# Two blocks in one launch: later request of half the tokens in the prologue, and results of the unnormed slabs taken after all normed eighths

## The chip, the cores and the metric

One core of one Trainium2 chip runs the kernel as a single program. The metric is the device time of one execution in microseconds (us); the lower the better. The core has five engines with queues of their own: PE (TensorE, the matmuls), DVE (VectorE), ACT (ScalarE), POOL (GpSimd) and SP (SyncE, which here only asks for transfers). They meet on semaphores alone.

## What is computed

Two transformer blocks over 512 tokens of width 1024, all in float32. The first has a gated causal convolution, an attention with three dilated windows and a gated feed-forward part. The second has a sparse-attention layer and a stick-breaking layer. The change touches the first norm and the first projection only:

```
h = rms_norm(x, norm1_g)              # x: 512 tokens x 1024
z = h @ w_in                          # 1024 x 7168
a_val, a_gate = z[:, :1024], z[:, 1024:2048]
a = a_val * sigmoid(a_gate)           # the "glu" part: 16 slabs of w_in
a = causal_depthwise_conv(a, conv_w, conv_b)      # 31 taps
...
```

## The kernel before

**Weights as a stream of slabs.** All weights come in one stream (`wstream`) of slabs of 128 x 1024 floats (512 KB), in the order in which they are used. A ring of four slots holds them in SBUF. A float32 product is made of three passes: each slab is kept as a high part `W_HI` and a remainder `W_LO`, and the activations likewise as `X_HI` and `X_LO`; the helper `mm3` issues high x high, high x low and low x high. For most slabs `W_HI` is loaded (POOL, L508), ACT or POOL writes its negative to `W_LO` (L1338 on ACT, function `negate`), and an accumulating transfer adds the slab again (POOL, L494), so that the remainder is left. `W_HI` of slab n may be asked for when slab n - 4 is done (`slab_done`).

**The tokens.** `X_T`, which shares its memory with `GATE_A` (so the profile says GATE_A), holds the tokens transposed: 1024 features as eight "eighths" k = 0..7 of 128 x 512. SP asks for them in four quarters of two eighths each (L454, 512 KB each), each with a semaphore of its own, `xt_in[0..3]`. The identity matrix (part of `CONST`, L453) is asked for just before the last quarter.

**The prologue.** The inverse norm of a token is known only when all tokens have come and their squares are summed. So that PE has work before that, the first four slabs (RAW = 4) are multiplied with unnormed tokens: ACT writes `RAW_HI` (= `O_HI`, L1324), DVE writes `RAW_LO` (= `O_LO`, L1887), and PE (`raw_slabs`, L946, L949, L954) leaves the results of slab n in PSUM bank n. These four slabs get their low parts from a second copy of the slab (`FIRST`, in `QKV[:, 2]`, L461 on SP) that DVE subtracts (L1915). ACT then squares the tokens (L1326), DVE adds the squares in pairs (L1894, L1925), PE sums over features (L970), and ACT, DVE and PE turn the sum into `INVERSE_NORM` (a part of `CONV_ROOT`).

**After the inverse norm is known** DVE has two jobs. One is per eighth: `x_normed(k)` (L1904) scales the eighth in place, ACT copies it to `X_HI` (L1343, `x_high`), and DVE subtracts to get `X_LO` (L1909, `x_low`). The other is per raw slab: `raw_tile(n)` (L1901) multiplies PSUM bank n by the inverse norm, stores it into `CONV` or `CONV_IN` and raises `tile_free`. Before the change the raw tiles stand between the eighths: tile 0 after eighth 3, tile 1 after eighth 5, tile 2 after eighth 7's scaling, tile 3 at the end.

**Slab 4 and on.** From slab 4 PE works on normed tokens (`f_phase("glu", ...)`, function `turn`, L521 to L523): eight eighths of three products each, with slab n in PSUM bank n mod 4. Before the first product of slab 4 it waits for bank 0, and before each eighth of slab 4 for that eighth of `X_LO`:

```
            pe.wait_ge(tile_free, t0 - upper if first else t0 + 4 * i + j - 3)
        for k in range(KT):
            if i == (1 if begun else 0) and j == 0:
                ready(k)            # x_lo >= k + 1
```

For slab 4 (i = 1, j = 0) the first wait is for one `tile_free` beyond the start value, and `raw_tile(0)` is what raises it.

**ACT's order at this place** is written by hand: negate slab 4, `X_HI` of eighths 0 and 1, negate slab 5, `X_HI` 2 to 5, negate slab 6, `X_HI` 6 and 7, then the sigmoids of raw tiles 0 and 2 (`raw_gate`, L1348), then negate slab 7:

```
            negate(SLOTS + 1)
            x_high(range(2, 6))
            negate(SLOTS + 2)
            x_high(range(6, KT))
            raw_gate(0)
            raw_gate(1)
```

`negate` waits until its slab has landed. After this place DVE runs the 31-tap convolution (L1968, L1972) beside PE's projections.

Of the kernel before, what the change touches and what calls it, by code (L numbers as in the profile page):

```python
# [110 lines left out]
RAW = 4  # L111
# [84 lines left out]
def program(nc, x, xt, wstream, consts, small, lnv, out):  # L196
    with ExitStack() as ctx:
# [5 lines left out]
        def sem(name):  # L203
            if name not in sems:
                sems[name] = ctx.enter_context(nc.semaphore(name))
            return sems[name]
# [198 lines left out]
        def o_part(k):  # L405
            return slice(k * P, (k + 1) * P)


        gains_in, small_in, const_in, xt_in = sem("gains_in"), sem("small_in"), sem("const_in"), [sem(f"xt_in{k}") for k in range(KT // 2)]
# [5 lines left out]
        def sml(name):  # L415
            return SMALLS[:, S_AT[name]]
# [30 lines left out]
        @block.sync  # L447
        def _(sp):
            sp.dma_start(sml("g1"), small[:, S_AT["g1"]]).then_inc(gains_in, 16)
            for k in range(KT // 2):  # L450
                if k == KT // 2 - 1:

                    sp.dma_start(ident, consts[:, C_AT["ident"]]).then_inc(xt_in[k], 16)  # L453
                sp.dma_start(X_T[:, 2 * k:2 * k + 2, :], xt[:, 2 * k * SEQ:2 * (k + 1) * SEQ]).then_inc(xt_in[k], 16)  # L454


            sp.wait_ge(xt_in[KT // 2 - 2], 16)
            for n in range(RAW):
                if n == 2:
                    sp.wait_ge(sem("first_in0"), 16)  # L460
                sp.dma_start(FIRST[:, n, :], wstream[n]).then_inc(sem(f"first_in{n}"), 16)  # L461
            sp.wait_ge(slab_done, 3)
            sp.dma_start(SMALLS[:, KT:], small[:, KT:]).then_inc(small_in, 16)

            for n in range(4):
                sp.wait_ge(slab_done, 8 + 6 * n)
                part = slice(P + n * (C_W - P) // 4, P + (n + 1) * (C_W - P) // 4)
                sp.dma_start(CONST[:, part], consts[:, part]).then_inc(const_in, 16)

            for k in range(KT):  # L470
                sp.wait_ge(sem("a_v_lo"), k + 1)
                sp.dma_start(X_AGAIN[:, :, o_part(k)], x[:, o_part(k)].rearrange("(t p) d -> p t d", p=P))\
                    .then_inc(sem("res_in"), 16)
            for t in range(TT):
                parts = 2 if t == TT - 1 else 1
                for n in range(parts):
                    c = slice(n * D // parts, (n + 1) * D // parts)
                    sp.wait_ge(sem("normed"), TT + t + n + 1)
                    sp.dma_start(out[t * P:(t + 1) * P, c], RESIDUAL[:, t, c]).then_inc(sem("stored"), 16)
            sp.wait_ge(sem("stored"), 16 * (TT + 1))  # L480
# [34 lines left out]
        def _(pe):  # L515
# [262 lines left out]
            def attention_out(_, last_scores, last_values, fill):  # L778
                s0, t0 = SLAB0["attn_out"], TILE0["attn_out"]

                def part(n, ks):
                    s = (s0 + n) % SLOTS
                    for k in ks:
                        w = slice(k * P, (k + 1) * P)
                        pe.wait_ge(sem("a_ol"), k + 1)
                        mm = mm3(PSUM[:, n, :], W_HI[:, s, w], W_LO[:, s, w], O_HI[:, :, o_part(k)], O_LO[:, :, o_part(k)],
                                 k == 0, k == KT - 1)
                    return mm

                fill(PAIRS, 0)  # L790
                last_scores()
                fill(PAIRS, 1)
                last_values()

                pe.wait_ge(sem("a_biased"), 8 * PAIRS)
                for n in range(KT):
                    if n == 2:
                        pe.wait_ge(tile_free, t0)
                    slab_ready(s0 + n)
                    part(n, range(KT)).then_inc(slab_done, 1)  # L800
# [821 lines left out]
        def _(dve):  # L1622
# [274 lines left out]
            def raw_tile(n):  # L1897

                dve.wait_ge(slab_done, n + 1)
                dst = CONV_IN[:, n // 2, CW - 1:] if n % 2 else CONV[:, n // 2, :]  # L1900
                dve.tensor_tensor(dst, PSUM[:, n, :], INVERSE_NORM, ALU.mult).then_inc(tile_free, 1)  # L1901

            def x_normed(k):
                dve.scalar_tensor_tensor(X_T[:, k, :], X_T[:, k, :], sml("g1")[:, k:k + 1], INVERSE_NORM,  # L1904
                                         ALU.mult, ALU.mult).then_inc(sem("x_normed"), 1)

            def x_low(k):
                dve.wait_ge(sem("x_hi"), k + 1)
                dve.tensor_tensor(X_LO[:, k, :], X_T[:, k, :], X_HI[:, k, :].bitcast(F32), ALU.subtract).then_inc(sem("x_lo"), 1)  # L1909
# [21 lines left out]
            for k in range(KT):  # L1931
                x_normed(k)
                if k:
                    x_low(k - 1)
                if k in (3, 5, 7):
                    raw_tile(k // 2 - 1)
            x_low(KT - 1)
            raw_tile(3)
            dve.wait_ge(small_in, 16)
            dve.tensor_scalar(half_gate_b[:, :], sml("gate_b"), 0.5, None, ALU.mult).then_inc(sem("filled"), 1)  # L1940

# [112 lines left out]
            for i in range(0, FT // 2):  # L2054
                for m in range(2):
                    for v in range(2):
                        b, n = 2 * m + v, 4 * m + 2 * v
# [340 lines left out]
```

## Time and profile before

| | us |
|---|---|
| median of 3 runs | 1546.37 (1546.09 to 1546.46) |
| the profiled execution | 1547.69 |
| its span, first to last instruction | 1545.8 |
| PE busy | 1513.5 (98%) |
| DVE busy | 927.6 (60%) |
| ACT busy | 525.5 (34%) |
| POOL busy | 539.9 (35%) |

The span is what the trace shows; the profiled execution's own time has 1.9 us around it. Busy times are unions of an engine's instructions. Matmuls are pipelined: one of 128 x 512 is shown 0.39 us long, and the next starts 0.23 us after it, so start times are the ones to read.

### The profile page before, as it was taken

The numbers are of one execution on the slowest core, as the hardware profiler recorded it, in microseconds if no ns is written. First come the engines' busy times: TensorE is split into PE (matmuls) and PEld (weight loads), VectorE is DVE, ScalarE is ACT, GpSimd is POOL, SyncE is SP. The second block draws the span as 40 slices with busy tenths as digits, with TensorE's granted clock in tenths as the row PEclk, the third lists the DMA queues.
The fourth block names the chain that finished last, engine by engine and source line by source line (L and its number), as shares of the span: only waits on it lengthen the run. The fifth ranks groups of instructions, "written<-read, shape, count | busy, mean of one in ns | idle before, by whom it ended". The sixth has DMA issues, their size and how long they took to land.

```text
span 1545.8 us, 19010 instructions
## 1 busy us (share of the span) xinstructions
PE 1513.5 (98%) x7390; PEld 1226.5 (79%) x7390; DVE 927.6 (60%) x1584; ACT 525.5 (34%) x1021; POOL 539.9 (35%) x654
## 2 busy tenths in 40 slices
PE   9999999999999999999999999999999989999996
PEld 7888888877788788888888887788777768778775
DVE  7999969378864334443410025896787351777765
ACT  5323334177741222222200012212777032444530
POOL 1222234411134444444444443344111344333221
PEclk9999999999999999999999999999999999999998
DMA  8999998844459888988888887788333768665655
GB/s 255 200 199 197 197 194 188 187 101 96 93 131 195 174 183 192 193 193 194 195 193 193 179 187 169 157 191 181 79 83 73 173 156 193 136 138 125 126 128 131
DMA packets 73689, 252.96 MB, mean 164 GB/s; under 512 B 7936, under 2 KB 12800, under 8 KB 73600
## 3 DMA queue, kind: packets, MB, share of 16 engines
q0 software_dynamic: 65952, 240.15, 71.9%
q1 hardware_dynamic: 7104, 9.50, 1.8%
q10 hardware_dynamic: 544, 2.10, 0.5%
q8 instruction: 59, 0.97, 0.3%
q14 instruction: 30, 0.25, 0.1%
HBM read 249.62 MB, written 2.10 MB: 163 GB/s over the span
## 4 chain that ended last, share of the span: by engine, by line
PE 90%; DVE 5%; DMA 3%; issue 1%; ACT 1%; POOL 0%; SPq 0%; DVEq 0%; ACTq 0%
PE PSUM L521 26%; PE PSUM L523 25%; PE PSUM L522 25%; PE PSUM L729 3%; PE PSUM L687 2%; PE PSUM L705 2%; DMA W_LO<-wstream 1%; PE PSUM L864 1%; PE PSUM L876 1%; DMA W_HI<-wstream 1%; PE PSUM L889 1%; PE PSUM L675 1%; PE PSUM L1066 1%; DVE PROBS L1694 1%; DVE HEAD_BIAS L1667 1%
## 5 line engine op out<-in xcount | busy, mean ns | idle before, releaser
L508 POOL DMA_DIRECT2D W_HI<-wstream x231 | 130.0, 563 | 844.7 <-PE PSUM L523 822.5
L521 PE MATMUL PSUM<-X_HI,W_HI 128*128 128x512 f32 x840 | 334.9, 399 | 1.1 <-DVE X_LO L1909 0.7
L523 PE MATMUL PSUM<-X_HI,W_LO 128*128 128x512 f32 x840 | 327.6, 390 | 0.0
L522 PE MATMUL PSUM<-X_LO,W_HI 128*128 128x512 f32 x840 | 327.6, 390 | 0.0
L494 POOL DMA_DIRECT2D W_LO<-wstream x227 | 204.2, 900 | 109.3 <-POOL W_LO L491 82.6
L521 PE MATMUL PSUM<-W_HI,X_HI 128*128 128x512 f32 x544 | 213.2, 392 | 2.9 <-DMA W_LO<-wstream 2.9
L491 POOL TENSOR_SCALAR W_LO<-W_HI 128x1024 fp32r<-128x1024 f32 x191 | 207.4, 1086 | 24.6 <-DMA W_HI<-wstream 21.3
L522 PE MATMUL PSUM<-W_LO,X_HI 128*128 128x512 f32 x544 | 211.8, 389 | 0.0
L523 PE MATMUL PSUM<-W_HI,X_LO 128*128 128x512 f32 x544 | 211.8, 389 | 0.0
L521 PEld LDWEIGHTS PSUM<-X_HI,W_HI 128*128 128x128 f32 x840 | 157.3, 187 | 42.7 <-issue 10.1
L523 PEld LDWEIGHTS PSUM<-X_HI,W_LO 128*128 128x128 f32 x840 | 157.4, 187 | 34.0
L522 PEld LDWEIGHTS PSUM<-X_LO,W_HI 128*128 128x128 f32 x840 | 157.5, 188 | 30.9
L1972 DVE SCALAR_TENSOR_TENSOR CONV<-CONV_IN,SMALLS,CONV 128x512 f32<-128x512 f32 x240 | 159.4, 753 | 0.0
L2066 DVE SCALAR_TENSOR_TENSOR GATE_A<-PSUM,SMALLS,GATE_A 128x511 f32<-128x511 f32 x88 | 65.9, 749 | 143.2 <-ACT GATE_A L1441 141.6
L521 PEld LDWEIGHTS PSUM<-W_HI,X_HI 128*128 128x128 f32 x544 | 102.1, 188 | 28.6 <-DMA W_LO<-wstream 3.7
L523 PEld LDWEIGHTS PSUM<-W_HI,X_LO 128*128 128x128 f32 x544 | 102.1, 188 | 21.3
L522 PEld LDWEIGHTS PSUM<-W_LO,X_HI 128*128 128x128 f32 x544 | 102.1, 188 | 20.8
L1441 ACT ACTIVATE GATE_A<-PSUM,SMALLS 128x512 f32<-128x512 f32 x44 | 34.3, 780 | 166.1 <-PE PSUM L523 165.4
L1195 ACT ACTIVATE PROBS<-PROBS,soft_stats 128x128 f32<-128x128 f32 (+3 forms) x128 | 71.0, 558 | 35.4 <-DVE soft_stats L1694 35.3
L1338 ACT ACTIVATE W_LO<-W_HI 128x1024 fp32r<-128x1024 f32 x36 | 38.2, 1061 | 124.9 <-DMA W_HI<-wstream 124.9
L521 PE MATMUL PSUM<-W_HI,FFN_HI 128*128 128x512 f32 x176 | 68.7, 390 | 0.0
L523 PE MATMUL PSUM<-W_HI,FFN_LO 128*128 128x512 f32 x176 | 68.5, 389 | 0.0
(253 smaller groups left out, 2402.7 us busy)
## 6 DMA issues: line engine op xcount, KB each, us to landing
W_HI<-wstream POOLq DMA_DIRECT2D x231, 512.0 KB, 3.9
W_LO<-wstream POOLq DMA_DIRECT2D x227, 512.0 KB, 5.6
GATE_A<-xt SPq DMA_DIRECT2D x4, 512.0 KB, 6.2
QKV<-wstream SPq DMA_DIRECT2D x4, 512.0 KB, 5.0
QKV<-x SPq DMA_DIRECT2D x8, 256.0 KB, 2.7
NORM_GAINS<-lnv ACTq DMA_DIRECT2D x2, 1024.0 KB, 6.7
out<-GATE_B SPq DMA_DIRECT2D x3, 512.0 KB, 2.6
CONST<-consts SPq DMA_DIRECT2D x4, 194.0 KB, 5.2
```

Source lines behind the costliest of these rows:

```text
L491: pool.tensor_scalar(W_LO[:, r, :], W_HI[:, r, :].bitcast(F32), -1.0, 0.0, ALU.mult, ALU.add)\
L494: pool.dma_start(W_LO[:, r, :], wstream[n], accum_op=ALU.add).then_inc(w_lo_in[r], 16)
L508: pool.dma_start(W_HI[:, n % SLOTS, :], wstream[n]).then_inc(w_hi_in[n % SLOTS], 16)
L521: pe.matmul(o, lh, rh, start=start, stop=False)
L522: pe.matmul(o, lh, rl, start=False, stop=False)
L523: return pe.matmul(o, ll, rh, start=False, stop=stop)
L729: mm = pe.matmul(PSUM[:, out_bank(a, i)[h], kb * P:], ATT_V[:, kb, h, :], part[:, h, r, :].rearrange("p b q -> p (b q)"), start=kb == 0 an ...
L1195: act.activation(p, p, ACT.Exp, scale=-1.0, bias=soft_stats[:, 0, q, h:h + 1], accum_out=soft_stats[:, 1 + i % 2, q, h:h + 1]).then_inc(se ...
L1338: act.activation(W_LO[:, r, :], W_HI[:, r, :].bitcast(F32), ACT.Copy, scale=-1.0).then_inc(sem("w_neg_act"), 1)
L1441: act.activation(FFN_CONV[:, 2 * m + v, :], PSUM[:, 2 * m + v, :], ACT.Identity, scale=SMALLS[:, bass.ds(i * 12 + (S_AT["fw"].start + (2 * ...
L1972: dve.scalar_tensor_tensor(acc, src, w, acc, ALU.mult, ALU.add).then_inc(step, 1)
L2066: ins = dve.scalar_tensor_tensor(FFN_CONV[:, b, d:], PSUM[:, b, 0:SEQ - d], w, FFN_CONV[:, b, d:], ALU.mult, ALU.add)
```

## The change

SP now waits for the first quarter of the tokens before it asks for the third; the identity and the fourth quarter stand behind that wait. On DVE the four raw tiles come after the last `x_low`.

```diff
@@ block.sync
             for k in range(KT // 2):
+                if k == 2:
+
+                    sp.wait_ge(xt_in[0], 16)
                 if k == KT // 2 - 1:
 
                     sp.dma_start(ident, consts[:, C_AT["ident"]]).then_inc(xt_in[k], 16)
@@ block.vector
                 x_normed(k)
                 if k:
                     x_low(k - 1)
-                if k in (3, 5, 7):
-                    raw_tile(k // 2 - 1)
             x_low(KT - 1)
-            raw_tile(3)
+            for n in range(RAW):
+                raw_tile(n)
```

The order of SP's first transfers before the change (`GATE_A<-xt` are the quarters, `CONST` the identity, `QKV<-wstream` the second copies of raw slabs):

```order
L449 DMA SMALLS<-small 128x8
L454 DMA GATE_A<-xt 128x1024 x3
L453 DMA CONST<-consts 128x128
L454 DMA GATE_A<-xt 128x1024
L461 DMA QKV<-wstream 128x1024 [waits xt_in2]
```

and of the change:

```order
L449 DMA SMALLS<-small 128x8
L457 DMA GATE_A<-xt 128x1024 x2
L457 DMA GATE_A<-xt 128x1024 [waits xt_in0]
L456 DMA CONST<-consts 128x128
L457 DMA GATE_A<-xt 128x1024
L464 DMA QKV<-wstream 128x1024 [waits xt_in2]
```

The same transfers are issued in the same order; the third has a wait. No other queue's order changes.

DVE's order from eighth 5 on, before the change (L1904 is `x_normed`, L1909 `x_low`, L1901 `raw_tile`):

```order
L1904 SCALAR_TENSOR_TENSOR GATE_A<-GATE_A,SMALLS,CONV_ROOT 128x512
L1909 TENSOR_TENSOR X_LO<-GATE_A,X_HI 128x512 [waits x_hi]
L1901 TENSOR_TENSOR CONV_IN<-PSUM,CONV_ROOT 128x512 [waits slab_done]
L1904 SCALAR_TENSOR_TENSOR GATE_A<-GATE_A,SMALLS,CONV_ROOT 128x512
L1909 TENSOR_TENSOR X_LO<-GATE_A,X_HI 128x512 [waits x_hi]
L1904 SCALAR_TENSOR_TENSOR GATE_A<-GATE_A,SMALLS,CONV_ROOT 128x512
L1909 TENSOR_TENSOR X_LO<-GATE_A,X_HI 128x512 [waits x_hi]
L1901 TENSOR_TENSOR CONV<-PSUM,CONV_ROOT 128x512 [waits slab_done]
L1909 TENSOR_TENSOR X_LO<-GATE_A,X_HI 128x512 [waits x_hi]
L1901 TENSOR_TENSOR CONV_IN<-PSUM,CONV_ROOT 128x512 [waits slab_done]
```

and of the change, from eighth 6 on (L1907 is `x_normed`, L1912 `x_low`, L1904 now `raw_tile`):

```order
L1907 SCALAR_TENSOR_TENSOR GATE_A<-GATE_A,SMALLS,CONV_ROOT 128x512
L1912 TENSOR_TENSOR X_LO<-GATE_A,X_HI 128x512 [waits x_hi]
L1907 SCALAR_TENSOR_TENSOR GATE_A<-GATE_A,SMALLS,CONV_ROOT 128x512
L1912 TENSOR_TENSOR X_LO<-GATE_A,X_HI 128x512 [waits x_hi] x2
L1904 TENSOR_TENSOR CONV<-PSUM,CONV_ROOT 128x512 [waits slab_done]
L1904 TENSOR_TENSOR CONV_IN<-PSUM,CONV_ROOT 128x512 [waits slab_done]
L1904 TENSOR_TENSOR CONV<-PSUM,CONV_ROOT 128x512 [waits slab_done]
L1904 TENSOR_TENSOR CONV_IN<-PSUM,CONV_ROOT 128x512 [waits slab_done]
```

`raw_tile(0)`, which stood before `x_normed` of eighth 4, now stands behind `x_low` of eighth 7. PE's order is the same before and after; the place where slab 4 begins on PE reads, in both but for line numbers:

```order
L521 MATMUL PSUM<-X_HI,W_HI 128x512 [waits x_lo,tile_free,w_lo_in0]
L522 MATMUL PSUM<-X_LO,W_HI 128x512
L523 MATMUL PSUM<-X_HI,W_LO 128x512
L521 MATMUL PSUM<-X_HI,W_HI 128x512 [waits x_lo]
L522 MATMUL PSUM<-X_LO,W_HI 128x512
```

Its first product waits for `tile_free`; nothing moved on PE itself.

## Rows read from the trace of the kernel before

**Rows 1.** The page: shares of the chain that ended last, by engine.
```profile
PE 90%; DVE 5%; DMA 3%; issue 1%; ACT 1%; POOL 0%; SPq 0%; DVEq 0%; ACTq 0%
```
**Rows 2.** Timeline of PE, 30 to 40.5 us (start, length, instruction, [idle before, releaser]).
```profile
30.77 1.98 PE L954 MATMUL PSUM<-O_HI,W_LO 128*128 128x512 f32 x8
32.58 0.39 PE L521 MATMUL PSUM<-X_HI,W_HI 128*128 128x512 f32 x1
...
36.43 0.39 PE L523 MATMUL PSUM<-X_HI,W_LO 128*128 128x512 f32 x1
37.27 0.50 PE L521 MATMUL PSUM<-X_HI,W_HI 128*128 128x512 f32 x1 [0.45 <-DVE X_LO L1909]
...
38.47 0.50 PE L521 MATMUL PSUM<-X_HI,W_HI 128*128 128x512 f32 x1 [0.24 <-DVE X_LO L1909]
...
39.27 0.39 PE L521 MATMUL PSUM<-X_HI,W_HI 128*128 128x512 f32 x1
```
**Rows 3.** Timeline of DVE, 24 to 41 us.
```profile
28.89 0.68 DVE L1901 TENSOR_TENSOR CONV<-PSUM,CONV_ROOT 128x512 f32<-128x512 f32 x1
...
36.52 0.69 DVE L1909 TENSOR_TENSOR X_LO<-GATE_A,X_HI 128x512 fp32r<-128x512 f32 x1 [1.89 <-ACT X_HI L1343]
37.13 0.69 DVE L1901 TENSOR_TENSOR CONV<-PSUM,CONV_ROOT 128x512 f32<-128x512 f32 x1
37.73 0.68 DVE L1909 TENSOR_TENSOR X_LO<-GATE_A,X_HI 128x512 fp32r<-128x512 f32 x1
...
39.60 1.29 DVE L1959 TENSOR_TENSOR CONV_IN<-CONV_IN,CONV 128x512 f32<-128x512 f32 x2 [0.51 <-ACT CONV L1348]
```
**Rows 4.** Timeline of ACT: the raw high parts, the squares, and the normed high parts.
```profile
7.58 3.93 ACT L1324 ACTIVATE O_HI<-GATE_A,SMALLS 128x512 fp32r<-128x512 f32 x6 [1.34 <-DMA GATE_A<-xt]
11.42 4.26 ACT L1326 ACTIVATE GATE_B<-GATE_A 128x512 f32<-128x512 f32 x8
...
34.91 1.06 ACT L1338 ACTIVATE W_LO<-W_HI 128x1024 fp32r<-128x1024 f32 x1 [2.74 <-DMA W_HI<-wstream]
35.87 1.14 ACT L1343 ACTIVATE X_HI<-GATE_A 128x512 fp32r<-128x512 f32 x2
```
**Rows 5.** Issues of slab 6's high part alone: count, KB, us from issue to landing.
```profile
W_HI<-wstream POOLq DMA_DIRECT2D x1, 512.0 KB, 7.2
```
**Rows 6.** Waits of PE over the whole span: waited for, us in total, times, longest.
```profile
PE PSUM L521 <- DMA W_LO<-wstream: 3.6, 3, 1.8
PE PSUM L811 <- DVE GATE_B L1845: 3.3, 1, 3.3
```
**Rows 7.** Waits of DVE from 40 to 300 us.
```profile
DVE QK_LO L1672 <- ACT QK_HI L1177: 18.1, 1, 18.1
DVE CONV_ROOT L1994 <- PE PSUM L996: 7.4, 1, 7.4
```
**Rows 8.** The four quarters of the tokens: us from issue to landing, least, median, most.
```profile
DMA to landing us min/median/max: 3.6/6.2/7.1
```
**Rows 9.** Stretches: PE, PEld, DVE, ACT, POOL busy, granted clock, DMA share, GB/s.
```profile
4.00:5.00 1.00, 1.00 (x7) 1.00 (x7) 0.00 (x0) 0.09 (x1) 0.00 (x0) 1.00 0.90 332
5.00:6.00 1.00, 1.00 (x11) 1.00 (x10) 0.33 (x1) 1.00 (x2) 0.00 (x0) 1.00 1.08 401
5.00:10.00 5.00, 3.86 (x23) 2.77 (x22) 3.07 (x5) 3.66 (x6) 0.55 (x1) 1.00 1.06 390
1536.00:1537.00 1.00, 0.00 (x0) 0.00 (x0) 0.96 (x3) 0.20 (x1) 0.00 (x0) 1.00 0.73 299
1537.00:1538.00 1.00, 0.00 (x0) 0.00 (x0) 0.96 (x3) 0.00 (x0) 0.00 (x0) 0.64 0.00 0
```
**Rows 10.** Timeline of SP and DVE in the prologue: quarters asked for, and the first squares added.
```profile
1.18 1.37 SPq L454 DMA_DIRECT2D GATE_A<-xt  x3
...
13.63 1.23 DVE L1894 TENSOR_TENSOR GATE_B<-GATE_B 128x1024 f32<-128x1024 f32 x1 [1.23 <-ACT GATE_B L1326]
```
**Rows 11.** The last matmul of the program.
```profile
1532.19 0.39 PE L523 MATMUL PSUM<-W_HI,O_LO 128*128 128x512 f32 x1
```

## Prediction

> **What bounds the kernel now.** I read the chain of the page first: 90% of the chain that ended last is PE [rows 1]. So a microsecond counts only where PE stands still, and PE's time lost once near the start is paid at the end unless a later wait takes it up. Next I read PE's timeline at the place of the change. PE ends the unnormed slabs at 30.77 + 1.98 = 32.75, and slab 4 begins at once, at 32.58 by start times; it runs six eighths, 18 products, and then stands briefly before eighths 6 and 7, which start at 37.27 and 38.47 [rows 2]. Slab 5 starts at 39.27. The spacing of products is (36.43 - 32.58) / 17 = 0.227 us.
>
> What holds eighths 6 and 7 is in the timelines of ACT and DVE. ACT is idle 2.74 us until slab 6 has landed, negates it at 34.91, and only then copies `X_HI` of 6 and 7 at 35.87 [rows 4]; slab 6's transfer took 7.2 us [rows 5]. DVE is idle 1.89 us for that copy, does `x_low(6)` at 36.52, raw tile 2 at 37.13 and `x_low(7)` at 37.73 [rows 3].
>
> **The change, part one: DVE's order.** Slab 4 writes bank 0, and PE may not begin it before `raw_tile(0)` has raised `tile_free`. Before, that tile ran at 28.89, 3.9 us ahead of need [rows 3]. Now it stands behind `x_low(7)`, which stands behind `x_low(6)`, which needs the ACT copy behind slab 6's landing. None of these waits for PE's slab 4, so nothing locks; PE stands. DVE now does `x_low(6)` at 36.52, `x_low(7)` at 37.13 and `raw_tile(0)` at 37.73, one step of 0.6 us each, as the three instructions there now [rows 3]. The tile takes the place of the old `x_low(7)`, after which PE started at 38.47; so PE starts slab 4 at about 38.47 too. Then come all 24 products, where before only three were left. The other 21 were done under the wait: 21 x 0.227 = **4.8 us** later. DVE is quicker through eighths 4 to 7 since tiles 0 and 1 are gone from between them (2 x 0.6 us), but that only makes it wait longer for ACT: worth nothing, and its cover is the landing of slab 6. Tiles 1, 2 and 3 follow at 0.6 us each, far ahead of slabs 5 to 7, which start 5.4 us apart. ACT's sigmoid of raw tile 2 waits for `raw_tile(2)`, now done some 1.2 us after 38.4, so negate of slab 7 and the convolution begin 0.8 to 0.9 us later; PE needs slab 7 only three slabs, 16 us, after slab 4's start, so that is hidden too.
>
> **Does it come back later?** PE's waits after this place are short and hang on things that PE itself released: the longest are 3.3 us for DVE at L811, and three for slabs (3.6 us in all), whose transfers are asked for when PE ends an earlier slab [rows 6]. The one long job that does not follow PE is the convolution on DVE; but DVE waits 7.4 us for PE behind it, and 18.1 us for ACT's copy of PE's result before the attention [rows 7], so PE was never waiting for it. Nothing absorbs the 4.8.
>
> **Part two: the later request.** Before, SP asks for three quarters in a row from 1.18 [rows 10]; the landings take 3.6 us for the first and 7.1 for the slowest [rows 8], so the first lands at about 4.8 and the fourth at 10.2. Now the third is asked for at about 4.9, the identity and the fourth behind it, at some 0.5 us each. ACT starts on the second quarter at 7.58, runs six copies without a break to 11.51, then the squares [rows 4], and DVE starts adding these at 13.63 after an idle 1.23 us [rows 10]. So the end of the raw copies passes one to one to everything behind it, slab 6's request included. Bounds: the best is that the second quarter lands as ACT ends the first, at 6.25, worth 1.3 us. The worst is that the third quarter again takes its median 6.2 us from the later request: it lands at 11.1 where ACT wants it at 7.58 + 1.31 = 8.9, a loss of 2.2. From the least transfer, 3.6 us, it lands at 8.5 and the fourth, asked for at 5.9, at 9.5, and nothing is lost. The row nearest is the traffic itself: between 5 and 10 us the engines move 390 GB/s at a full share [rows 9], and the same quarters and slab 0 (2.7 MB with the identity) must all go through before the fourth has landed. Holding two back does not make fewer bytes; and the second stood ahead of them on SP's queue already. I take **0**, with +-0.8.
>
> The Trainium skill (DMA: Bandwidth & Descriptors, Queues, rings and completion order) says that an engine consumes a ring's descriptors in order and goes round between the rings that have work. By that rule the held-back quarters could not have delayed the second, which is on the same ring, but only slab 0 on POOL's: PE's first product would start earlier, and the end of the copies would not move. It speaks against the change's first half, and the rows do not contradict it.
>
> **The clock.** PE would stand from 32.75 to 38.48, 5.7 us. The trace has two rows to set beside it: an idle 3.3 us at L811 [rows 6], where the granted clock stayed at full speed, and the end of the program. There the last matmul ends at 1532.58 [rows 11], the clock is still full between 1536 and 1537, and the mean of 0.64 in the next us [rows 9] says that it fell to 1.2 GHz 0.28 us into it: 4.7 us after the last matmul. A stand of 5.7 us is beyond that one fall, so I think a fall likelier than none. Its price: after the start the warm-up matmuls go at 7 a us until 5 us and at 11 then [rows 9], so the slow stretch was some 4 us after the first at about 1.1. Four us at half speed cost 2.0 us; if up to 1.0 us of the low clock (5.7 - 4.7) lies in the stand, 3 us are left, 1.5. Bounds 0.5 and 3 (the stretch at 1 us, or at 6). I take **1.5**.
>
> The Trainium skill (TensorE: Matmul & The Clock Gate, HAM oscillation) describes just this: a PE that waits for data between bursts is throttled and begins each burst at half rate. By it the time is 1.5 us longer than by the 3.3 us row, where nothing fell; the end of this trace agrees.
>
> **Sum.** 4.8 + 0 + 1.5 = 6.3 us on the profiled execution's 1547.69, so 1554.0. That execution is 1.3 us above the median of the runs; the delay is the same in both, so the forecast is 1546.37 + 6.3 = **1552.7 us**.
>
> **Rivals.** (a) *The stand without the fall of the clock.* For it: only one fall is in the trace, and 5.7 is not far beyond 4.7. Then 1546.37 + 4.8 = 1551.2. Chance 0.3.
> (b) *The later request works or hurts by much.* If the second quarter came 1.3 us earlier and the rest in time, the prologue gives back 1.3: 1551.4 with the fall, 1549.9 without. If the third comes late by 2.2, 1554.9. Against: the full traffic of [rows 9]. Both lie in the range; chance 0.06 together beyond what I allow above.
> (c) *Slab 6 lands early, and the result is not slower.* The stand is set by slab 6's 7.2 us. If it took 3.6 us, the least that 512 KB took in the prologue, ACT would be free for 6 and 7 as soon as DVE has scaled them, and `raw_tile(0)` would follow DVE's own chain: the last scaling ended at 36.52 - 1.89 = 34.6 [rows 3], now 1.2 sooner, at 33.4; three steps of 0.6 end at 35.2, and slab 4 ends 24 products on, at 40.7 instead of 39.3. That is +1.4, less up to 1.3 from the request: 1546.5 to 1547.8, within 0.2%. It decides from a landing some 2 us sooner. It ends faster by over 0.2% (over 3.1 us, about what a measurement can tell from no change) only if something else in the prologue shortens as well. Against it: the same accumulating transfers of slabs 4 and 5 run beside slab 6 in both orders. Chance 0.04 within, 0.02 faster.
> (d) *The order does not do what it says*, another semaphore releasing bank 0. DVE's tiles are the only ones that raise `tile_free` before slab 4, and PE's first product names it. I give it nothing of its own; it is in the 0.02 to 0.04 of (c).
>
> **Chances.** Forecast 0.58, (a) 0.3, (b) 0.06, (c) 0.06. The range reaches from (a) with 0.8 us of gain, 1550.4, to the forecast with a slow stretch of 5 us and a late quarter, 1554.6; that leaves (c) and the worst end of (b) out. Slower by over 0.2% (above 1549.5): 0.94; within 0.2%: 0.04; faster: 0.02.
>
> **What would show it.** PE idle once for 5 to 6 us before its first L521, released by DVE's L1904 tile; 24 products in a row after it without the two short stands; slab 5 starting near 44 instead of 39.27; a granted clock below 1.00 in the stretch around 36 to 42, and product spacing of about 0.45 us there, if the fall comes. ACT's squares starting at 11.4, give or take 0.8, would show that the request is worth nothing. Everything behind should be the old timeline, shifted. I am wrong if PE starts slab 4 before 36, if the shift at slab 5 is gone by 300 us, or if the squares move by over 1.5 us.

## The result, and the profile after

| | us |
|---|---|
| before, median | 1546.41 (4 runs, 1546.09 to 1546.68) |
| changed, median | 1555.62 (4 runs, 1555.08 to 1559.44) |
| ratio, 95% interval | 1.0063 (1.0050 to 1.0076) |
| the profiled execution, its span | 1555.32, 1553.4 |

The change is slower by 9.2 us, 0.6%. The forecast was 6.3 us slower, with a range up to 1554.6: the direction and the place were right, the size was not, and the result lies 1.0 us outside. Between the two profiled executions the difference is 7.6 us (1547.69 and 1555.32): that of the kernel before lies 1.3 us above its median, that of the change 0.3 under its own.

The page of the changed kernel: busy times, and the chain by engine. Against before PE is busy 4 us longer in a span 7.6 us longer, so part of the loss is PE standing and part is PE running slower.

```profile
PE 1517.6 (98%) x7390; PEld 1229.9 (79%) x7390; DVE 927.3 (60%) x1584; ACT 525.6 (34%) x1021; POOL 540.1 (35%) x654
...
PE 90%; DVE 5%; DMA 2%; issue 1%; ACT 1%; POOL 0%; SPq 0%; DVEq 0%; ACTq 0%
```

PE's timeline of the changed kernel around the start of slab 4 (L524 to L526 are what L521 to L523 were), which answers to [rows 2]:

```profile
32.26 1.98 PE L957 MATMUL PSUM<-O_HI,W_LO 128*128 128x512 f32 x8
38.84 0.72 PE L524 MATMUL PSUM<-X_HI,W_HI 128*128 128x512 f32 x1 [4.61 <-issue]
39.36 0.63 PE L525 MATMUL PSUM<-X_LO,W_HI 128*128 128x512 f32 x1
...
41.92 0.58 PE L525 MATMUL PSUM<-X_LO,W_HI 128*128 128x512 f32 x1
42.34 0.39 PE L526 MATMUL PSUM<-X_HI,W_LO 128*128 128x512 f32 x1
...
45.97 0.39 PE L524 MATMUL PSUM<-X_HI,W_HI 128*128 128x512 f32 x1
```

One stand of 4.6 us, then 24 products in a row, the first eight 0.43 us apart and the others 0.23. Slab 5 starts at 45.97 where it started at 39.27: 6.7 us later. The profile puts the stand's end down to "issue"; what ended it is in DVE's timeline of the same kernel (L1912 `x_low`, L1904 `raw_tile`), to be read beside [rows 3]:

```profile
36.84 1.29 DVE L1912 TENSOR_TENSOR X_LO<-GATE_A,X_HI 128x512 fp32r<-128x512 f32 x2 [1.88 <-ACT X_HI L1346]
38.06 0.68 DVE L1904 TENSOR_TENSOR CONV<-PSUM,CONV_ROOT 128x512 f32<-128x512 f32 x1
38.66 0.68 DVE L1904 TENSOR_TENSOR CONV_IN<-PSUM,CONV_ROOT 128x512 f32<-128x512 f32 x1
```

Raw tile 0 runs from 38.06 to 38.74, and PE starts at 38.84. DVE itself had waited 1.88 us for ACT, and ACT for slab 6. ACT's timeline of the changed kernel, beside [rows 4]:

```profile
8.30 2.72 ACT L1327 ACTIVATE O_HI<-GATE_A,SMALLS 128x512 fp32r<-128x512 f32 x4 [1.89 <-DMA GATE_A<-xt]
11.18 1.34 ACT L1327 ACTIVATE O_HI<-GATE_A,SMALLS 128x512 fp32r<-128x512 f32 x2 [0.16 <-DMA GATE_A<-xt]
12.43 4.26 ACT L1329 ACTIVATE GATE_B<-GATE_A 128x512 f32<-128x512 f32 x8
...
35.24 1.06 ACT L1341 ACTIVATE W_LO<-W_HI 128x1024 fp32r<-128x1024 f32 x1 [2.13 <-DMA W_HI<-wstream]
```

The squares start 1.0 us later than before (12.43 against 11.42): the second quarter came 0.7 us later (8.30 against 7.58) and the fourth once more let ACT wait. The 0.7 us need not come from the change: in e13 below, where the tokens are asked for as before, ACT starts on the second quarter at 8.48. Slab 6's negation starts 0.3 us later (35.24 against 34.91).

Stretches of the changed kernel (PE, PEld, DVE, ACT, POOL busy, granted clock, DMA share, GB/s):

```profile
38.00:39.00 1.00, 0.16 (x1) 0.19 (x2) 1.00 (x3) 0.86 (x2) 0.00 (x0) 0.95 1.11 242
39.00:42.00 3.00, 3.00 (x8) 2.32 (x9) 2.88 (x7) 1.98 (x3) 0.00 (x0) 0.50 0.76 141
42.00:43.00 1.00, 1.00 (x5) 0.82 (x4) 1.00 (x4) 0.00 (x0) 0.00 (x0) 0.85 0.09 20
...
1247.00:1254.00 7.00, 5.79 (x18) 4.91 (x19) 4.35 (x8) 2.27 (x5) 2.93 (x3) 0.52 0.94 202
```

The clock fell to half, 1.2 GHz, at 38.9, after PE had stood since 34.24, and was back 3.4 us later; slab 4 took 7.1 us where 24 products at 0.227 take 5.4. There is a second stretch at half clock that was not in the profile of before: around 1247 to 1254, around the end of the stand of 3.3 us in a late norm, which is as long as it was [rows 6].

The 6.7 us at slab 5 are thus made of 0.4 for the start (38.84, foreseen at 38.47), 4.6 for the products (24 x 0.227, less the 0.8 us that the last three took before) and 1.7 for the clock. From there to a stand of PE near 1183 us (1190 in the change) both kernels take 1143.7 us, and behind it the change loses another 0.9.

### The profile page after: what moved, and what is told of

Its sections match the earlier page's. It is cut to its first block, busy times and chain, and to the rows that moved or that the text cites. A ratio compares the mean times of both kernels' runs of the same rounds, so it can differ in the third digit from the quotient of the medians.

```text
span 1553.4 us, 19010 instructions
## 1 busy us (share of the span) xinstructions
PE 1517.6 (98%) x7390; PEld 1229.9 (79%) x7390; DVE 927.3 (60%) x1584; ACT 525.6 (34%) x1021; POOL 540.1 (35%) x654
## 4 chain that ended last, share of the span: by engine, by line
PE 90%; DVE 5%; DMA 2%; issue 1%; ACT 1%; POOL 0%; SPq 0%; DVEq 0%; ACTq 0%
PE PSUM L524 26%; PE PSUM L525 25%; PE PSUM L526 25%; PE PSUM L732 3%; PE PSUM L690 2%; PE PSUM L708 2%; PE PSUM L867 1%; PE PSUM L879 1%; PE PSUM L892 1%; PE PSUM L678 1%; DMA W_LO<-wstream 1%; DMA W_HI<-wstream 1%; PE PSUM L1069 1%; DVE PROBS L1697 1%; DVE HEAD_BIAS L1670 1%
## 5 line engine op out<-in xcount | busy, mean ns | idle before, releaser
L524 PE MATMUL PSUM<-X_HI,W_HI 128*128 128x512 f32 x840 | 335.5, 399 | 5.0 <-issue 4.6
L526 PE MATMUL PSUM<-X_HI,W_LO 128*128 128x512 f32 x840 | 328.1, 391 | 0.0
L524 PE MATMUL PSUM<-W_HI,X_HI 128*128 128x512 f32 x544 | 214.3, 394 | 1.4 <-DMA W_LO<-wstream 1.1
L526 PE MATMUL PSUM<-W_HI,X_LO 128*128 128x512 f32 x544 | 212.5, 391 | 0.0
L524 PEld LDWEIGHTS PSUM<-X_HI,W_HI 128*128 128x128 f32 x840 | 157.7, 188 | 46.6 <-issue 15.1
L526 PEld LDWEIGHTS PSUM<-X_HI,W_LO 128*128 128x128 f32 x840 | 157.8, 188 | 34.0
L524 PEld LDWEIGHTS PSUM<-W_HI,X_HI 128*128 128x128 f32 x544 | 102.7, 189 | 27.5 <-issue 3.3
L526 PEld LDWEIGHTS PSUM<-W_HI,X_LO 128*128 128x128 f32 x544 | 102.5, 188 | 21.6
L524 PE MATMUL PSUM<-W_HI,FFN_HI 128*128 128x512 f32 x176 | 68.7, 390 | 0.0
L525 PE MATMUL PSUM<-W_LO,FFN_HI 128*128 128x512 f32 x176 | 68.5, 389 | 0.0
```

The costliest lines, as they stand in the source:

```text
L524: pe.matmul(o, lh, rh, start=start, stop=False)
L525: pe.matmul(o, lh, rl, start=False, stop=False)
L526: return pe.matmul(o, ll, rh, start=False, stop=stop)
```

## The experiments

The experiments ran in four groups (e1 to e4, e5 to e8, e9 to e12, e13 to e16), each on one chip. The kernel before ran again in each group, and its medians were 1549.95, 1548.98, 1548.51 and 1548.05 us, with runs from 1545.6 to 1552.9; its first four runs, within 0.6 us, were at the low end of that. Each difference below is against the kernel before of the same group. With such a spread a median of 11 or 12 runs is good to 1 to 2 us, one of 5 or 6 runs to about 2, and a single profile shows one execution, not the typical one.

### e1: the later request alone

```diff
             for k in range(KT // 2):
+                if k == 2:
+
+                    sp.wait_ge(xt_in[0], 16)
```

> The kernel before with the later request of the third and fourth quarter alone. In the profile of the change the third unnormed slab was done 1.5 us later than before (slab 6 asked for at 29.18 against 27.69), but slab 6 landed only 0.33 us later. Theory A (the late prologue is hidden by slab 6's landing): +0.2 to +0.5 us, 1546.6 to 1546.9. Rival B (what the prologue loses is paid in full): +1.5 us, 1547.9. The forecast had it at nothing: 1546.4.

Measured: 1550.85 (12 runs) against 1549.95, +0.9, ratio 1.0009 (0.9998 to 1.0020). The median lies between A and B, and the interval holds zero. The profiled execution shows more: slab 5 starts at 42.37, 3.1 us later than in [rows 2]. PE's timeline and a stretch of e1:

```profile
12.96 0.50 PE L952 MATMUL PSUM<-O_LO,W_HI 128*128 128x512 f32 x1
15.28 0.50 PE L949 MATMUL PSUM<-O_HI,W_HI 128*128 128x512 f32 x1 [1.82 <-DMA W_HI<-wstream]
```
```profile
16.00:19.00 3.00, 3.00 (x10) 2.28 (x9) 3.00 (x4) 0.07 (x1) 0.77 (x2) 0.54 0.88 274
```

PE waits 1.8 us for slab 1, which landed at 15.2 (asked for at 8.36, 6.9 us), and the clock falls behind that stand. So slab 5 can be several microseconds late in one execution, while the median hardly moves.

### e2: DVE's order alone

```diff
-                if k in (3, 5, 7):
-                    raw_tile(k // 2 - 1)
             x_low(KT - 1)
-            raw_tile(3)
+            for n in range(RAW):
+                raw_tile(n)
```

> The kernel before with all four raw tiles behind the last x_low, tokens asked for as before. Theory A (the stand of PE is the whole thing): 4.8 us for 21 products no longer done under the wait, and 1.5 to 2 us if the clock falls in the stand of 5.7 us; slab 5 starts 6.3 to 6.7 us later; with a second fall at the layer norm near 1248 us, one more: 1552.7 to 1554.1. Rival B (half of the 9.2 us come from the late request): under 1551.5.

Measured: 1557.83 (5 runs) against 1549.95, +7.9, ratio 1.0052 (1.0040 to 1.0065). PE in e2's profile:

```profile
38.53 0.47 PE L521 MATMUL PSUM<-X_HI,W_HI 128*128 128x512 f32 x1 [4.58 <-issue]
```

The same stand, and a fall of the clock 0.7 us behind its end: slab 5 starts at 45.70, 6.4 us late. The order carries most of the loss. The 7.9 us are above both theories' numbers; e15 repeats it.

### e3: raw tile 0 left in its place, the others behind

```diff
-                if k in (3, 5, 7):
-                    raw_tile(k // 2 - 1)
+                if k == 3:
+                    raw_tile(0)
             x_low(KT - 1)
-            raw_tile(3)
+            for n in range(1, RAW):
+                raw_tile(n)
```

> The kernel before with raw tile 0 where it was, after the eighth 3, and only tiles 1 to 3 behind the last x_low. Theory A (only tile 0's place costs, since bank 0 is what slab 4 waits for): no stand of PE before slab 4, and x_low of eighth 7 one step of 0.6 us earlier since tile 2 no longer stands before it: -0.5 us, 1545.9. Rival B (the move of the tiles costs by itself, through slabs 5 to 7 or the later convolution): +0.5 us or more.

Measured: 1549.53 (12 runs) against 1549.95, -0.4, ratio 1.0003 (0.9993 to 1.0013), no difference. In its profile PE has no stand before slab 4, and slab 5 starts here:

```profile
38.93 0.39 PE L521 MATMUL PSUM<-X_HI,W_HI 128*128 128x512 f32 x1
```

That is 0.3 us before [rows 2]. It is one tile, the one that frees bank 0, that costs the time; the move of the other three costs nothing that these runs can tell.

### e4: the change, with PE kept busy in its stand

```diff
                 high(3, range(KT))
                 low(3)
+                for n in range(26):
+                    pe.matmul(PSUM[:, 7, 0:P], ONES, ONES, start=True, stop=True)
```

> The change with 26 matmuls of 128 x 128 on the matrix of ones into the unused bank 7 behind the last unnormed slab, some 4.7 us of work in a stand of 4.6 to 5.7 us, so that PE is busy there. Theory A (1.6 to 2 us of the change is the clock falling in the stand): no fall near 39 us, product spacing 0.227 from the start of slab 4, 1.4 to 2.0 us under the change, 1553.6 to 1554.2; the later fall near 1247 may come or go with the shift. Rival B (the slow first products of slab 4 are something else): 1555.6 as the change.

Measured: 1556.13 (5 runs) against 1549.95, +6.2. By its median this is theory B's number, but the kernel before, too, is 3.5 us higher in this group than in its first runs; the profile decides. PE and DVE in its profile:

```profile
33.48 5.96 PE L987 MATMUL PSUM<-QK_SQ 128*128 128x128 f32 x52
39.20 0.48 PE L524 MATMUL PSUM<-X_HI,W_HI 128*128 128x512 f32 x1
39.52 0.40 PE L525 MATMUL PSUM<-X_LO,W_HI 128*128 128x512 f32 x1
```
```profile
37.27 0.69 DVE L1906 TENSOR_TENSOR CONV<-PSUM,CONV_ROOT 128x512 f32<-128x512 f32 x1
```

The products run at full speed at once, so the slow first products of the change are the clock. But I had made the filling too long: raw tile 0 ended at 37.96 and PE came back only at 39.20, so this kernel pays 1.2 us for its own filling. Without that I estimate +5.0 (6.2 - 1.2).

### e5: the kernel before, once more

> The kernel before, once more, for a profile on the chip of this call. In the last call its runs went from 1546.0 to 1552.9 where the first four were within 0.6 us. Theory A (the spread is slab 1's landing in the prologue, 12.0 us in the first profile and 13.8 to 15.2 in three of the last four, and the clock falling in short stands that it survives in other runs): a span over 1546 comes with slab 1 after 13.5 us or with a granted clock of 0.50 somewhere between 10 and 1530 us. Rival B (this chip is slower throughout): the stretches between are longer, with neither.

Measured: 1549.62 (8 runs), the profiled one 1548.80 with a span of 1546.9. Two stretches of it:

```profile
536.00:539.40 3.40, 3.40 (x18) 3.30 (x17) 2.89 (x5) 3.00 (x6) 1.01 (x2) 0.50 0.97 261
1242.00:1246.20 4.20, 3.08 (x12) 2.85 (x13) 3.79 (x8) 2.18 (x5) 2.70 (x3) 0.59 0.88 182
```

The unchanged kernel has the clock falling too: behind two stands of 0.8 and 1.0 us in the norm near 535, and behind the 3.3 us one. In the first profile neither fell. Slab 1 landed at 14.0 instead of 12.0, and slab 5 started at 39.29 all the same. Theory A holds for this execution: 1.7 us are gone by 545 us, at the first of the falls.

### e6: the change again

The kernel is the change, as it was.

> The change on the chip of this call, for a comparison without a change of chip. Theory A (the stand with its clock is 6.5 to 7 us, the rest of the first 9.2 us was chance of the runs): 6.5 to 7.5 us over the kernel before. Rival B (9 us belong to the change on any chip): 8.5 us or more over it.

Measured: 1556.89 (6 runs) against 1548.98, +7.9, ratio 1.0056 (1.0041 to 1.0071). Between the theories. It is the +7.9 of e2 again, so this pair, from two groups, gives nothing to the request; e13 to e16 put both in one group. The stand ends at 38.17, slab 5 starts at 45.34, 6.05 us after e5's.

### e7: the kernel before with ACT's last two high parts ahead of slab 6's negation

```diff
-            x_high(range(2, 6))
-            negate(SLOTS + 2)
-            x_high(range(6, KT))
+            x_high(range(2, KT))
+            negate(SLOTS + 2)
```

> The kernel before with ACT's high parts of eighths 6 and 7 ahead of the negation of slab 6, so that they do not wait for its landing. Theory A (what holds eighths 6 and 7 is ACT's place behind slab 6): no stand of PE at 37 to 38 us, slab 5 starts 1.2 us earlier, 1.2 us under the kernel before. Rival B (DVE's own chain holds them): no gain over 0.3 us.

Measured: 1549.19 (12 runs) against 1548.98, nothing (0.9991 to 1.0008). PE in its profile at the start of slab 5, and 17 us later:

```profile
38.45 0.39 PE L521 MATMUL PSUM<-X_HI,W_HI 128*128 128x512 f32 x1
...
55.77 0.50 PE L521 MATMUL PSUM<-X_HI,W_HI 128*128 128x512 f32 x1 [0.84 <-DMA W_LO<-wstream]
```

Slab 5 is 0.84 us earlier than in e5, so A was right about what holds the eighths, and then PE waits 0.84 us for a slab's remainder at slab 8. In this execution the gain was given back to the stream of weights. The interval reaches from 1.4 us faster to 1.2 slower, so a part of the gain in other runs is not ruled out.

### e8: the change with the same move on ACT

> The change with the same move on ACT. Theory A (the stand's length is set by slab 6's landing by way of ACT): raw tile 0 ends some 1.9 us earlier, PE's stand is 2.7 us instead of 4.6 and the clock does not fall in it: 1.9 us, with the clock 3.5 us, under the change of this call. Rival B (the stand is set by DVE's chain of the eighths alone): the stand stays at 4.6 us and the time at the change's.

Measured: 1554.62 (6 runs) against 1548.98, +5.6, and 2.3 us under e6. PE in its profile:

```profile
36.74 0.47 PE L524 MATMUL PSUM<-X_HI,W_HI 128*128 128x512 f32 x1 [2.78 <-issue]
```

The stand is 2.8 us, as expected, and the clock does not fall in it (slab 4 takes 5.53 us). The length of the stand is set by slab 6's landing by way of ACT. The profiled execution, 1551.68, is the fastest of the six, 2.9 us under their median; what the clock did in the stands of the others is not known.

### e9 and e12: no falls in the later norms

e9 is the kernel before and e12 the kernel of e3, both with

```diff
                         if c == 0:
+                            for n in range((0, 0, 3, 4)[t]):
+                                pe.matmul(PSUM[:, 0, t * P:(t + 1) * P], ident, ident, start=True, stop=True)
                             pe.wait_ge(sem("x_scaled"), scaled + t + 1)
...
                 if t == 2:
+                    pe.wait_ge(tile_free, TILE0["out_a"] + 5)
+                    for n in range(12):
+                        pe.matmul(PSUM[:, 4, 0:P], ident, ident, start=True, stop=True)
                     pe.wait_ge(tile_free, TILE0["out_a"] + 8)
```

> The kernel before with extra matmuls of 128 x 128 on the identity, into parts of banks that are overwritten next, where PE stands in the later norms: 3 and 4 of them before the last two tokens' turns of the norm near 534 us (stands of 0.77 and 0.98 us), 12 in the stand of 3.3 us near 1240 us. Theory A (the runs of the kernel before that lie above 1546.5 lie there because the clock falls after these stands): no fall at 536 or 1243, the median 1.5 to 3 us under the kernel before of this call, and a narrower spread, near 1546. Rival B (the spread comes from transfers): the median and the spread as before.

> The kernel of e3 (raw tile 0 in its place, tiles 1 to 3 behind the last x_low) with the extra matmuls of e9. Theory A (x_low of eighth 7 one step of 0.6 us earlier): 0.3 to 0.5 us under e9, and so the fastest of all. Rival B (PE reaches eighth 7 no sooner than before because the unnormed slabs end later in most runs): the same as e9 within 0.3.

Measured: e9 1548.61 (11 runs) and e12 1547.89 (11 runs) against 1548.51; ratios 0.9999 (0.9990 to 1.0007) and 0.9999 (0.9991 to 1.0008). My theory A of e9 fell. The clock stays up at both places, in the profile and, by its mean of 0.996 to 0.997, in all eleven runs, and the time is the same. Stretches of e9, and its waits of PE for slabs beside those of e5:

```profile
536.00:539.40 3.40, 3.40 (x23) 3.00 (x22) 3.31 (x6) 3.40 (x8) 0.90 (x1) 1.00 1.00 263
1242.00:1246.20 4.20, 4.20 (x25) 3.65 (x26) 3.16 (x6) 1.16 (x2) 2.06 (x2) 1.00 1.03 250
```
```profile
PE PSUM L521 <- DMA W_LO<-wstream: 4.5, 4, 1.9
```
```profile
PE PSUM L521 <- DMA W_LO<-wstream: 1.8, 3, 1.0
```

With the falls PE waits 1.8 us for slabs, without them 4.5. Nearly all of these waits lie between 1225 and 1277 us, just before and behind the late norm. Over all 18 profiles, the nine in which the clock falls at that norm wait 1.6 to 2.8 us there, the nine others 2.4 to 4.6. So PE runs against the stream of weights there, and loses to it a part of what it does not lose to the clock. e12 against e9 is -0.7, less than what these runs can tell. No kernel of the study is measurably faster than the one before.

### e10 and e11: the change and the request, without falls in the norms

e11 is e1 with the edit of e9. e10 is the change with it, and with 17 in place of e4's 26 matmuls.

> The change with the same extra matmuls, and 17 on the ones in its stand before slab 4 (3.9 us, ending before raw tile 0). Theory A (without the clock the change costs only the 21 products that no longer run under the wait): 4.8 to 5.5 us over e9, restart at the end of raw tile 0, spacing 0.227 at once. Rival B (the change costs more by something other than the clock): 7 us or more over e9.

> The later request alone with the extra matmuls of e9. Its first profile had PE's slab 4 end 3.1 us later than before, after slab 1 landed at 15.2 and the clock fell at 16.2 in the stand of 1.8 us before it. Theory A (the request moves the landing of the tokens by 0.4 to 1 us and slab 1's with it, and slab 6's landing hides some): 0.5 to 1.5 us over e9. Rival B (the 3.1 us are what it costs each time): 3 us over e9. Rival C (nothing): within 0.3 of e9.

Measured: e10 1555.01 (5 runs) against 1548.51, +6.5, 6.4 over e9; e11 1549.27 (12 runs), 0.7 over e9. e11 agrees with A and with e1, though its interval (0.9996 to 1.0016) holds zero. e10 is between its two theories, and in its profile slab 1 landed at 15.2, PE stood 1.2 us for it, the clock fell, and slab 6 landed at 37.5; so the prologue that the filling was meant to leave alone was late.

### e13 to e16: request and clock, two by two, on one chip

All four have DVE's new order. e13 is e10 without the later request, e14 is e10, e15 is e2, e16 is the change.

> DVE's new order alone, tokens asked for as before, with the extra matmuls of e10 (17 in the stand before slab 4, 3, 4 and 12 in the later norms). Theory A (stand 5 us, clock in it some 1.7, request some 0.8): 5.0 to 5.5 us over the kernel before of this call, 0.5 to 1.2 under e14. Rival B (the request adds nothing once the stand is there): as e14.

> The kernel of e10 again, beside the other three of this call. Theory A: 5.8 to 6.5 us over the kernel before, 1.5 to 2 under e16.

> The kernel of e2 again. Theory A: 6.7 to 7.5 us over the kernel before, a fall of the clock near 39 us in the profile. Rival B (e2's 7.9 us hold, so that the request adds nothing): 7.9 and as e16.

> The change a third time. Theory A: the sum of the three, 7.5 to 8.3 us over the kernel before; 0.5 to 1.2 over e15.

| over the kernel before (1548.05, 18 runs) | tokens asked for as before | later request | |
|---|---|---|---|
| PE kept busy | e13: +3.9 (11 runs) | e14: +4.8 (7 runs) | request +0.9 |
| PE left to stand | e15: +5.5 (6 runs) | e16: +9.0 (6 runs) | request +3.5 |
| | clock +1.6 | clock +4.2 | |

All four missed what theory A named: e13, e14 and e15 came out 1.0 to 1.2 us under it and e16 0.7 over it, so that e16 is 3.5 us over e15 where 0.5 to 1.2 were expected. Only the 3.5 and the 4.2 stand out of the spread: five of e15's six runs and all of e14's lie under the fastest of e16, 1554.99, while the ranges of e13 and e14 overlap widely.

Nor is the 3.5 to be taken for the size of the request: e2 and e6, the same two kernels as e15 and e16, are both at +7.9. And the filling stands only before slab 4 and in the later norms, so it does not spare e14 a fall behind slab 1; that none came there is the chance of that execution (in e10, the same kernel, it came).

How the request can add is in e16's profile (1559.61, the slowest of its six), PE's timeline and stretches:

```profile
13.57 0.50 PE L952 MATMUL PSUM<-O_LO,W_HI 128*128 128x512 f32 x1
15.36 0.72 PE L949 MATMUL PSUM<-O_HI,W_HI 128*128 128x512 f32 x1 [1.29 <-DMA W_HI<-wstream]
...
41.38 0.76 PE L524 MATMUL PSUM<-X_HI,W_HI 128*128 128x512 f32 x1 [4.55 <-issue]
```
```profile
16.00:19.00 3.00, 3.00 (x9) 2.35 (x8) 3.00 (x4) 0.84 (x2) 0.86 (x2) 0.52 0.86 283
39.00:46.00 7.00, 4.62 (x11) 3.68 (x12) 6.49 (x12) 4.37 (x6) 0.86 (x1) 0.53 0.81 169
1251.00:1258.00 7.00, 5.62 (x18) 4.78 (x19) 4.60 (x8) 2.44 (x5) 2.94 (x4) 0.51 0.99 208
```

Slab 1 is late (15.3), PE stands 1.3 us for it with the clock falling behind, so the third unnormed slab is done 4 us later than before, slab 6 is asked for at 31.8 instead of 27.7 and lands at 37.8, raw tile 0 follows, and slab 4 starts at 41.4, at half clock again. In e14's profile the clock is full from 34 to 44 and slab 4 takes 5.55 us:

```profile
38.73 0.47 PE L524 MATMUL PSUM<-X_HI,W_HI 128*128 128x512 f32 x1 [0.65 <-issue]
```

In e13's profile the stand before slab 4 is filled up to its last 0.8 us, and slab 5 starts at 43.69:

```profile
38.16 0.47 PE L521 MATMUL PSUM<-X_HI,W_HI 128*128 128x512 f32 x1 [0.80 <-issue]
...
43.69 0.39 PE L521 MATMUL PSUM<-X_HI,W_HI 128*128 128x512 f32 x1
```

Its trace has no separate stretches of the clock, only one mean of 0.95 for nearly all of it; that the clock did not fall before slab 4 is read off the products, which come 0.23 us apart from the second one on.

All profiles together, nine with the later request (the change, e1, e4, e6, e8, e10, e11, e14, e16) and nine without:

| | asked for as before | later request |
|---|---|---|
| slab 1 landed, us (mean) | 12.0 to 14.1 (13.2) | 13.0 to 15.3 (14.5) |
| slab 6 landed, us (mean) | 33.8 to 34.9 (34.4) | 34.4 to 38.0 (35.9) |
| clock fell at 15 to 16 us | in none | in three (e1, e10, e16) |

Slab 4's start follows slab 6's landing: in all eight profiles of DVE's new order with ACT's old order and no filling beyond raw tile 0 (the change, e2, e6, e10, e13 to e16) it comes 3.6 us after it. And the whole of an execution can be put together from pieces, of which the first carries what these kernels differ in (us; markers are two stands of PE that every profile has, near 1183 and near 1476 in the kernel before; from the second to the end all take 69.6 to 70.1):

| | slab 5 starts | to the stand near 1183 | on to the one near 1476 | clock low at the late norm |
|---|---|---|---|---|
| before | 39.27 | 1143.7 | 293.3 | 0 |
| the change | 45.97 | 1143.7 | 294.2 | 6.8 |
| e2 | 45.70 | 1143.6 | 295.6 | 6.8 |
| e6 | 45.34 | 1143.6 | 295.3 | 6.8 |
| e15 | 45.07 | 1144.0 | 292.7 | 3.4 |
| e16 | 49.16 | 1143.6 | 295.4 | 6.8 |

The middle piece is 1143.4 to 1144.0 in 13 of the 18 profiles; in the four with a fall near 540 us (e1, e4, e5, e7) it is 1145.3 to 1146.3, and in e13 1145.1. The last piece goes from 292.4 to 295.7 whatever the kernel: 294.9 in the mean of the six profiles with 6.8 us of low clock at the late norm, 293.4 in the six without any fall after 1183 us, and 293.2 in the three with 3.4 us. So e2 and e15, one kernel, are 0.6 us apart at slab 5 and 3.2 at the end. At slab 5 the profiles give the request 1.4 us in the mean over DVE's new order without filling (-0.1, 0.6 and 3.8 us).

## Why the prediction was right and wrong

**Part one, the order: right.** "21 x 0.227 = **4.8 us** later" for the products that no longer run under the wait, with raw tile 0 taking the place of the old `x_low(7)`. In e13's profile, without the request and the fall, slab 5 starts at 43.69, which is 4.4 to 4.9 us after the kernels without a stand (39.29 in e5, 38.81 in e9), and e13 costs 3.9 us. e3 shows that it is tile 0 alone, e8 that the cover is slab 6's landing, as the text had it. The tail terms (tiles 1 to 3, ACT's sigmoid, the convolution) were nothing, as said: the piece from slab 5 to 1183 us is as long as before. One reading is loose: tile 0 had stood "3.9 us ahead of need" by its start, and its end was 3.0 ahead.

**Nothing gives it back: right up to 1183 us.** From slab 5 to there both kernels take 1143.7 us. What I had not seen is the stretch behind it, where the stream of weights takes up part of what PE gains or loses, and where executions of one kernel part by up to 3 us.

**Part two, the request: the first term that failed.** I took "**0**, with +-0.8", on the argument that the same bytes must pass at 390 GB/s before the fourth quarter has landed. That counted the quarters and stopped there. The fourth quarter did come later (ACT starts on it at 11.2 against 10.2 in the first two profiles), and the squares at 12.43 fall outside the "11.4, give or take 0.8" that was to show that the request is worth nothing, though 0.7 of that delay need not be the request's. The next transfer is later too: slab 1, by 1.2 us in the mean of nine profiles each. That it shares the engines with the late quarters and with the copies for DVE is my reading; no run shows it by itself. And I let the shift end at the squares, though the text itself had said that it passes to slab 6's request: since raw tile 0 now hangs on slab 6, 3.6 us before slab 4, the 1.5 us by which that lands later in the mean go on to slab 4 in full. In the execution of the result it was only 0.4; in e16's, 3. Over the runs the request costs 0.7 to 0.9 us alone (e11, e1; neither interval is clear of zero), 0.9 on top of the stand with PE kept busy, and 3.5 (e16 over e15) or nothing (e6 and e2, both +7.9) without. That it is more than nothing is shown by the landings and by e16; its size stays open between 0 and 3.5.

**The clock: the mechanism right, the reason for it not, and the price too small.** "A stand of 5.7 us is beyond that one fall", of 4.7 us, was why I took a fall for likely. In the five profiles of the new order without filling and with ACT as it was (the change, e2, e6, e15, e16) the stand was 4.5 to 4.6 us long, shorter than 4.7, since PE ended the unnormed slabs later than in [rows 2] or, in e15, slab 6 landed sooner; and the clock fell in every one, 2.2 to 5.3 us after PE had stopped (35.1 after 32.9 in e15, 39.2 after 33.9 in e2). So that the fall came was partly luck. "I take **1.5**": slab 4 takes 7.1 to 7.2 us instead of 5.5 in three of the profiles, 1.6 to 1.7 more, and 7.7 and 7.8 in two, 2.2 more. Keeping PE busy is worth 1.6 us in one pair (e15 over e13) and 4.2 in the other (e16 over e14); slab 4 itself is 2.2 us longer without it in the profiles of both pairs (7.7 and 7.8 us against 5.5), so the medians do not settle the size. What I had not priced at all are the other falls: the one behind slab 1's stand (e1, e10, e16), and the one at the late norm, which is there in all five of these profiles and not in the first of the kernel before, and costs about 1.5 us where it lasts 6.8 (an estimate, from the means of the last piece: 294.9 against 293.4). I had put one number on one fall in one place, when its chance was to be asked at every short stand.

**Where the 2.9 us of the miss lie.** Of 9.2 measured against 6.3, 0.4 had come about at slab 5 (6.7), 0.9 more behind 1183 us, where the second fall is, and 1.6 are the difference between the two profiled executions and the two medians. That last part is no term of the sum but the base, 1546.37, which the later runs of the same kernel do not bear out.

**The rivals.** (a), a stand without a fall, is e13 and e14 by construction, and no profiled execution without filling. (b) named the late request, with a loss of at most 2.2 and 0.06 of the chance; it deserved more, in the form it took. It also said that its ends "lie in the range", but 1554.9 and 1549.9 lie outside 1550.4 to 1554.6. (c) did not come about; e8 is as near to it as an edit got, and still 5.6 us slower. Of the trace's marks these came as listed: one stand released by the tile, 24 products in a row, a spacing of 0.43. The stand was 4.6 us long, not "5 to 6", and slab 5 started at 45.97, not "near 44".

**The level.** The first four runs of the kernel before lay at 1546.1 to 1546.7, where 93 later ones in four groups went from 1545.6 to 1552.9 around 1549. The change's first four (1555.6) agree with its later medians (1556.9, 1557.0). Against those groups the loss is 7.9 and 9.0. Why the first runs of before were so even is open. The spread that e9 keeps without falls of the clock in the norms lies, by the profiles, mostly behind 1183 us, in the piece that takes 292.4 to 295.7 us; what makes it long or short beyond the clock is open too.

## What to carry to other kernels

A wait that gates the first product of a phase is not like one that gates its eighth: before a step is moved behind others, look who needs its semaphore first, and what the others in turn are waiting for. A transfer moved by two microseconds is to be followed to the transfers that are asked for after it, not only to its own landing, and above all to the one that ends the stand. And a stand of PE is to be priced twice, by its length and by the clock that comes back late, with a chance for it at each stand, short ones too. And where two profiles of one kernel end 3 us apart, common stands of an engine, taken as markers, tell in which stretch they part.

## What the runs showed of the hardware

The clock can fall behind short stands. It fell to half at stands of 1.2, 1.3 and 1.8 us for slab 1 (e10, e16 and e1, in e16 with PE paced by DVE in the microseconds ahead of it) and behind two of 0.8 and 1.0 us close together (e5), each time for 3.4 us; stands of 0.8 to 1.1 us for slab 1 (e2, e3, e5, e6, e11) left it up. The same stand of 3.3 us near 1240 us left it up in the first profile of the kernel before and in e1, and let it fall in e5, e3, the change and others, for 3.4 or 6.8 us. In e14, where that stand was filled, it fell all the same, at 1256.4, behind a wait of 1.8 us for a slab. So the same instructions at the same places get another clock from one execution to the next. The Trainium skill (TensorE: Matmul & The Clock Gate, What's actually happening) says that the window in which activity is judged runs free of the kernel; the falls that come and go agree with that.

A slab of 512 KB asked for by POOL at about 8 us landed after 3.9 to 7.3 us in 18 profiles, asked for between 7.8 and 8.9, with the same transfers around it but for when the quarters were asked for. A sum that takes such a landing from one profile has a term of 3 us in it that may be another the next time.
